# Row products that end quarter by quarter, in a two-block transformer layer on one core

## The reference

```python
# first block
mix = concat([o_a, o_b]) @ w_out
x = x + gate1 * mix
h2 = modulate(rms_norm(x, norm2_gain), shift2, scale2)
y = peer(h2, ...)              # ends in (gates * act) @ expert_up, a sum over 16384 experts
x = x + gate2 * y
# second block
h = rms_norm(x, norm1_gain); proj = h @ w_in; ...
mixed = sigmoid(ga) * (o_hg @ w_hg_out) + sigmoid(gb) * (o_sb @ w_sb_out)
x = x + mixed @ w_o
h2 = rms_norm(x, norm2_gain)
gate, up = split(h2 @ w_ffn_in)
x = x + (silu(gate) * up) @ w_ffn_out
```

## Time and profile before

| | |
|---|---|
| time, median of 3 runs | 1680.39 us (1679.71 to 1683.46) |
| the profiled execution | 1681.05 us, of which its span 1679.3 us |
| PE busy | 1586.3 us, 94% of the span |
| DVE busy | 1226.5 us, 73% |
| ACT busy | 907.7 us, 54% |
| mean granted TensorE clock | 0.979 of full speed |

### The profile page before, as it was taken

How to read it: one execution, slowest core, us unless ns; L and a number is a source line. 1 busy time by engine, 2 the same in 40 slices (tenths; PEclk the granted TensorE clock), 3 DMA queues, 4 the chain that set the end, 5 groups by cost and what they waited for, 6 DMA issues and landing times. The chain is left out here.

```text
span 1679.3 us, 26490 instructions
## 1 busy us (share of the span) xinstructions
PE 1586.3 (94%) x10351; PEld 1426.4 (85%) x10351; DVE 1226.5 (73%) x2476; ACT 907.7 (54%) x1519; POOL 42.7 (3%) x82
## 2 busy tenths in 40 slices
PE   5988889999999999999999999899999899889998
PEld 5976767999999999978888888797888677789997
DVE  5876766889997999957767777657887566654564
ACT  5765455545545555545555555556555756455453
POOL 0022000000000000000000000020000000000000
PEclk9999999999999999999999999999999899999999
DMA  9943354576666454567788777645343223445552
GB/s 322 368 148 115 101 176 132 177 236 231 224 218 206 148 165 149 167 219 241 246 283 289 253 240 239 224 160 167 126 151 126 76 90 111 149 151 178 178 199 101
DMA packets 111664, 313.85 MB, mean 187 GB/s; under 512 B 9440, under 2 KB 10040, under 8 KB 102072
## 3 DMA queue, kind: packets, MB, share of 16 engines
q1 hardware_dynamic: 100008, 276.95, 49.7%
q10 hardware_dynamic: 11040, 33.66, 5.9%
q0 software_dynamic: 496, 1.59, 0.3%
HBM read 293.28 MB, written 18.89 MB: 186 GB/s over the span
## 5 line engine op out<-in xcount | busy, mean ns | idle before, releaser
L300 PE MATMUL ps<-parts,parts 128*128 128x512 f32 (+1 forms) x4992 | 972.7, 357 | 21.1 <-DVE parts L290 15.0
L300 PEld LDWEIGHTS ps<-parts,parts 128*128 128x128 f32 x4992 | 825.7, 192 | 156.1 <-DVE parts L290 15.4
L285 ACT CAST parts<-lead 128x512 fp32r<-128x512 f32 x940 | 579.8, 621 | 618.8 <-PE ps L300 398.5
L290 DVE TENSOR_TENSOR parts<-lead,parts 128x512 fp32r<-128x512 f32 x940 | 641.1, 689 | 330.0 <-ACT parts L285 326.3
L1817 PE MATMUL ps<-parts,parts 128*128 128x256 f32 x3072 | 385.3, 285 | 4.6 <-DVE parts L290 4.6
L1817 PEld LDWEIGHTS ps<-parts,parts 128*128 128x128 f32 x3072 | 372.6, 192 | 5.6 <-DVE parts L290 5.6
L376 PE MATMUL ps<-lead,mem 128*128 128x128 f32 (+2 forms) x292 | 45.5, 319 | 44.9 <-ACT mem L519 23.4
L376 PEld LDWEIGHTS ps<-lead,mem 128*128 128x128 f32 (+2 forms) x292 | 39.8, 159 | 52.6 <-ACT mem L519 24.8
L1994 DVE TENSOR_SCALAR mem<-lead,mem 128x128 f32<-128x128 f32 x256 | 71.0, 340 | 0.0
L1803 PE MATMUL ps<-mem 128*128 128x128 f32 x512 | 67.8, 275 | 0.7 <-DVE mem L1994 0.7
L1803 PEld LDWEIGHTS ps<-mem 128*128 128x128 f32 x512 | 62.8, 192 | 1.1 <-issue 1.1
(11 more groups left out here) (349 smaller groups left out, 999.5 us busy)
## 6 DMA issues: line engine op xcount, KB each, us to landing
lead<-in_peer_expert_down SPq DMA_DIRECT2D x64, 1024.0 KB, 5.5
lead<-in_peer_expert_up SPq DMA_DIRECT2D x64, 1024.0 KB, 6.0
lead<-in_w_in SPq DMA_DIRECT2D x50, 1024.0 KB, 5.1
lead<-in_w_ffn_in SPq DMA_DIRECT2D x22, 1024.0 KB, 5.2
act_spill<-mem ACTq DMA_DIRECT2D x32, 512.0 KB, 5.1
mem<-act_spill ACTq DMA_DIRECT2D x32, 512.0 KB, 3.6
mem<-in_w_ada SPq DMA_DIRECT2D x29, 512.0 KB, 7.5
lead<-in_w_ffn_out SPq DMA_DIRECT2D x11, 1024.0 KB, 4.9
```

The lines of the kernel that those rows point to most:

```text
L285: act.copy(w_hi[g % BUFFERS], st.words(n, u * UNIT, UNIT)).then_inc(hi_ready, 1)
L290: dve.tensor_tensor(w_lo[g % BUFFERS], st.words(n, u * UNIT, UNIT), w_hi[g % BUFFERS].bitcast(F32), ALU.subtract).then_inc(lo_ready, 1)
L300: mm = pe.matmul(o, lhs[a], rhs[b], start=start and i == 0, stop=stop and i == 2, skip_group_check=True, **kw)
```

## The change

A new function `last_units` runs the last 4 units of all five products. It first waits for all four units (`ready`), then does the products in another order: token tile 0, column half 0 (units 0 and 2 of the four); tile 0, half 1 (units 1 and 3); tile 1, half 0; tile 1, half 1. `s_rows` counts the first three quarters, and `unit_used` reaches its last value with the fourth. The second and third of the four buffers are given back together. DVE waits for each quarter and works on 512 columns at a time. `half_roots` replaces `norm_roots` in the three places with a norm: it squares each quarter; the sum of a row's first half, over 1024 and plus the epsilon, becomes the bias of that row tile's root (one small Identity), whose input is the sum of the second half. There is one root for each token tile in place of one for both. ACT waits for its own square and Identity each time. The result is stored in four DMAs of 128 rows x 512 columns in place of two of 128 x 1024.

```diff
+        def half_roots(act, rows, src, s_sq, s_src):
+            steps = 0
+            for tt in range(TT):
+                first, second, base, root = (tiny[:, 8 + 2 * i + tt:9 + 2 * i + tt] for i in range(4))
+                for c, total in enumerate((first, second)):
+                    act.wait_ge(s_src, 2 * tt + c + 1)
+                    act.activation(half_of(rows, tt, c), half_of(src, tt, c), ACT.Square, accum_out=total).then_inc(s_sq, 1)
+                    steps += 1
+                    act.wait_ge(s_sq, steps)
+                    if c == 0:
+                        act.activation(base, first, ACT.Identity, bias=eps, scale=1.0 / D).then_inc(s_sq, 1)
+                        steps += 1
+                one = act.activation(tiny[:, 2 + tt:3 + tt], second, ACT.Sqrt, bias=base, scale=1.0 / D)
+            return one
+
+        def half_of(v, tt, c):
+            return v[:, tt, c * 512:(c + 1) * 512]
+
+        def last_units(pe, ready, half, n, s_rows):
+            order = (0, 2, 1, 3)
+            for i in range(n - 4, n):
+                ready(i)
+            for m, i in enumerate(order):
+                mm = half(n - 4 + i, 0)
+                if m % 2:
+                    mm.then_inc(s_rows, 1)
+            for m, i in enumerate(order):
+                mm = half(n - 4 + i, 1)
+                if m != 1:
+                    mm.then_inc(unit_used, (1, 0, 2, 1)[m])
+                else:
+                    mm.then_inc(s_rows, 1)
...
-                    for i in range(units - 4, units):
+                    def ready(i):
                         if turn and i % 2 == 0:
                             turn.await_k(pe, i // 2)
                         await_unit(pe, g0 + i, 0)
-                        mm = half(i, 0)
-                    mm.then_inc(s_rows, 1)
-                    for i in range(units - 4, units):
-                        half(i, 1).then_inc(unit_used, 1)
+
+                    last_units(pe, ready, half, units, s_rows)
...
                     for tt in range(TT):
-                        if tt == 0:
-                            dve.wait_ge(s_rows, 1)
-                        else:
-                            dve.wait_ge(unit_used, used_value(g0 + units - 1))
-                        dve_part(dve, step, tt)
+                        for c in range(2):
+                            if tt == 0 or c == 0:
+                                dve.wait_ge(s_rows, 2 * tt + c + 1)
+                            else:
+                                dve.wait_ge(unit_used, used_value(g0 + units - 1))
+                            dve_part(dve, step, tt, c)
...
-        def add_mix(dve, step, tt):
-            step(dve.tensor_tensor(at(O_TMP + tt * D, D), product_rows(tt), gate1, ALU.mult))
-            dve.tensor_tensor(x[:, tt, :], x[:, tt, :], at(O_TMP + tt * D, D), ALU.add).then_inc(s_xsum, 1)
+        def add_mix(dve, step, tt, c):
+            gated, o = at(O_TMP + tt * D + c * 512, 512), half_of(x, tt, c)
+            step(dve.tensor_tensor(gated, product_half(tt, c), gate1[:, c * 512:(c + 1) * 512], ALU.mult))
+            dve.tensor_tensor(o, o, gated, ALU.add).then_inc(s_xsum, 1)
...
                 for tt in range(TT):
-                    sp.wait_ge(s_res, tt + 1)
-                    sp.dma_start(out[0, tt * P:(tt + 1) * P, :], x[:, tt, :]).then_inc(s_out, 16)
-                sp.wait_ge(s_out, 16 * TT)
+                    for c in range(2):
+                        sp.wait_ge(s_res, 2 * tt + c + 1)
+                        sp.dma_start(out[0, tt * P:(tt + 1) * P, c * 512:(c + 1) * 512], half_of(x, tt, c)).then_inc(s_out, 16)
+                sp.wait_ge(s_out, 16 * 2 * TT)
```

More of the change, by code:

```diff
@@ L1556, in _, with product_half @@
                     for tt in range(TT):
-                        if tt == 0:
-                            dve.wait_ge(s_rows, 1)
-                        else:
-                            dve.wait_ge(unit_used, used_value(g0 + units - 1))
-                        dve_part(dve, step, tt)
+                        for c in range(2):
[4 more added lines that the diff above has]
+                            dve_part(dve, step, tt, c)
         def product_rows(tt, j=0):
             return psf[:, j * 2048 + tt * D:j * 2048 + (tt + 1) * D]
+        def product_half(tt, c, j=0):
+            return ps[:, 4 * j + 2 * tt + c, :]
         O_TMP = O_C
         s_xsum, s_xsq = sem("x1_rows"), sem("x1_squares")
-        def add_mix(dve, step, tt):
-            step(dve.tensor_tensor(at(O_TMP + tt * D, D), product_rows(tt), gate1, ALU.mult))
-            dve.tensor_tensor(x[:, tt, :], x[:, tt, :], at(O_TMP + tt * D, D), ALU.add).then_inc(s_xsum, 1)
+        def add_mix(dve, step, tt, c):
+            gated, o = at(O_TMP + tt * D + c * 512, 512), half_of(x, tt, c)
+            step(dve.tensor_tensor(gated, product_half(tt, c), gate1[:, c * 512:(c + 1) * 512], ALU.mult))
+            dve.tensor_tensor(o, o, gated, ALU.add).then_inc(s_xsum, 1)
         def sum_roots(act):
             load_roots(act)
-            norm_roots(act, h, x, s_xsq, s_xsum)
+            half_roots(act, h, x, s_xsq, s_xsum)
         s_cols = sem("mods_added")
@@ L1846, in _ @@
                         transposes(pe, [(ps[0:KT, 0, 0:P], mod_cols[:, 5 * KT:6 * KT])]).then_inc(s_gt, 1)
[L1847 to L1852, removed]
+                last_units(pe, lambda i: await_unit(pe, g1 + i, 0), half, 2 * P, s_rows)
             @block.scalar
@@ L2053, in _ @@
                 for tt in range(TT):
[L2054 to L2059, removed]
+                    for c in range(2):
+                        if tt == 0 or c == 0:
+                            dve.wait_ge(s_rows, 2 * tt + c + 1)
+                        else:
+                            dve.wait_ge(unit_used, used_value(g1 + 2 * P - 1))
+                        o = half_of(x, tt, c)
+                        step(dve.tensor_tensor(o, product_half(tt, c, 1), gate2[:, c * 512:(c + 1) * 512], ALU.mult))
+                        dve.tensor_tensor(o, o, half_of(x_back, tt, c), ALU.add).then_inc(s_xsum, 1)
         O_F = O_R + TT * D
@@ L2751, in mix_hg, with add_sb @@
                 step(dve.tensor_tensor(mixed[:, tt, :], product_rows(tt), p2[:, tt, 5 * D:6 * D], ALU.mult))
-        def add_sb(dve, step, tt):
-            step(dve.tensor_tensor(at(O_W + 2048, D), product_rows(tt), p2[:, tt, 6 * D:7 * D], ALU.mult))
-            step(dve.tensor_tensor(mixed[:, tt, :], mixed[:, tt, :], at(O_W + 2048, D), ALU.add))
+        def add_sb(dve, step, tt, c):
+            gated, o = at(O_W + 2048 + c * 512, 512), half_of(mixed, tt, c)
+            step(dve.tensor_tensor(gated, product_half(tt, c), p2[:, tt, 6 * D + c * 512:6 * D + (c + 1) * 512], ALU.mult))
+            step(dve.tensor_tensor(o, o, gated, ALU.add))
         rows_stage("w_sb", n_sbo, 4, n_wo[0] + SLOTS, (x_hi, x_lo), add_sb, Turn("heads", p2[:, :, 2 * D:3 * D]),
@@ L2761, in build, with add_wo @@
         s_xsum, s_xsq = sem("x3_rows"), sem("x3_squares")
-        def add_wo(dve, step, tt):
-            dve.tensor_tensor(x[:, tt, :], x[:, tt, :], product_rows(tt), ALU.add).then_inc(s_xsum, 1)
+        def add_wo(dve, step, tt, c):
+            o = half_of(x, tt, c)
+            dve.tensor_tensor(o, o, product_half(tt, c), ALU.add).then_inc(s_xsum, 1)
         rows_stage("w_o", n_wo, 4, n_ffi[0] + SLOTS, (x_hi, x_lo), add_wo, Turn("mixed_rows", mixed), sum_roots)
@@ L2816, in _ @@
                     half(i, 1).then_inc(unit_used, 1)
[L2817 to L2822, removed]
+                last_units(pe, ready, half, FU, s_rows)
             @block.scalar
@@ L2884, in _ @@
                 for tt in range(TT):
[L2885 to L2889, removed]
+                    for c in range(2):
+                        if tt == 0 or c == 0:
+                            dve.wait_ge(s_rows, 2 * tt + c + 1)
+                        else:
+                            dve.wait_ge(unit_used, used_value(g_o + FU - 1))
+                        o = half_of(x, tt, c)
+                        dve.tensor_tensor(o, o, product_half(tt, c, 1), ALU.add).then_inc(s_res, 1)
 NAMES = ["x", "c", "w_ada", "b_ada", "norm1_gain", "w_in", "attn_q_gain", "attn_k_gain", "attn_rel_bias",
```

## The result

The changed kernel takes 1684.64 us (median of 20 runs, 1683.25 to 1690.12) against 1682.6 us for the kernel before in as many runs (1678.74 to 1685.81). The ratio is **1.0023**, 95% interval 1.0015 to 1.0032: slower, by 3.9 us (2.5 to 5.4). The forecast was +2.8 us and called it no measurable difference. Its edge for that was 0.2%, 3.4 us; the 3.9 lies just beyond it, and the interval takes in both sides. The time of 1684.64 lies in the whole range of the forecast (1679.6 to 1685.2) and 0.1 us outside the forecast's own (to 1684.5). That it lies so near is in part luck: the forecast stands on three runs of the kernel before with a median of 1680.39, and twenty runs have 1682.6.

A forecast was written before the change was run, and what follows sets the result against it. PE, busy 94% of the span, was taken as the bound. Stalls of 8.65 us against 5.33 given back made +3.3, less 0.5 for the clock: 1680.39 + 2.8 = 1683.2 us, own range 1681.0 to 1684.5, whole range 1679.6 to 1685.2.

The forecast's parts named there:

- The stall: At all five product ends, PE waits for the last unit before the last 24 matmuls: 1.73 us each, 8.65 us added.
- the restart: At each product end, PE resuming and the way to the waiting engine take 0.40 us, of which 0.38 was counted.
- The gains: From T to the next stage at five ends, smaller takes, squares, roots and stores give back 5.33 us in all.
- T: The moment at which DVE can take the last rows of a product; forecast to come 1.73 us later.
- The store: End of w_ffn_out: the last store, 256 KB in place of 512 KB, lands 0.5 us sooner, bounds 0 and 1.0.
- The clock: PE's granted clock in the gaps after products: the fall after w_o goes away, so 0.5 us comes back.
- the two long ones: PE's gaps after w_out and expert_up, forecast at 4.8 us each: the clock still falls, costing 1.6 us each.
- the one of 3.8: PE's gap after w_o, forecast to shrink from 4.8 to 3.8 us: the clock rather doesn't fall, 0.5 us back.
- Rival 4: The stall itself lowers the clock in the last 24 matmuls at any one place: up to +5.4 us; chance 0.07.
- Rival 3: At the five product ends the stall costs nothing: 1674.6 us, 0.35% faster; chance 0.06.
- Rival 1: The clock falls at the same three places as before (w_out, expert_up, w_o): 1683.7 us; chance 0.22.
- Rival 2: The clock stays up after w_out or expert_up too: 1681.6 us for one, 1680.0 for both; chance 0.24.

## Why the prediction was nearly right in size and wrong in its verdict

*The stall (forecast 8.65 us for five).* Right in kind and place, a little small. From split to last take it is 7.25 at w_out and 7.36 at w_ffn_out where 7.17 was forecast: four stalls of 1.8 and one of 1.92, 9.1 in all. Each lies above the forecast's upper bound of 1.75. What was mis-sized is the restart, 0.40 at most by the forecast and 0.46 (1.81 less 1.35) here. PE resumes 0.15 us after DVE's low part at w_out and 0.26 at w_ffn_out (1673.63 to 1673.89), where a further wait, for the low parts of the other operand, follows the awaited one; in the earlier trace rows it was 0.05.

*The gains (forecast 5.33).* They were 5.9. The root after w_out ends at T + 2.49 and not T + 2.71, since a following DVE operation starts before its predecessor's recorded end, so that DVE keeps PE's pace; At w_o the root ends at T + 1.77 where T + 1.75 was forecast. The store gave 0.6 for 0.5.

*The sum.* Both errors cancel: +3.3 forecast, +3.24 by the table; that it is so close is luck.

*The clock (forecast: 0.5 us back).* This is the step that failed. "I expect the two long ones to fall still, and the one of 3.8 rather not": the clock fell after w_o as before, and of the 0.5 us only 0.2 came back there (from the first split behind w_o to the last of w_ffn_out 1672.29 - 1485.99 = 186.30 us, before 186.49). And after w_sb, where the forecast had the clock stay up because 2.3 is less than 3.0, and so put nothing into the sum, it fell, for 1.2 us. The forecast judged a gap by its length alone. The runs show that length alone does not decide: 2.25 us behind the early wait brought the clock down in each execution and 2.28 without it in none, and an unchanged gap of 3.1 us did so in seven of twelve. Why the early wait has this effect stays open, as said above. Rival 4 named the stall as a cause of a fall, but looked for it inside the last 24 matmuls; it came one gap later. The Trainium skill (TensorE: Matmul & The Clock Gate, Part 1: The HAM clock gate) ties the clock to how busy PE has been of late and has the moment of a change vary from run to run; the unchanged gap with and without a fall agrees with that.

With the fall the ends come to 3.24 + 1.2 = 4.4 us, inside the measured 2.5 to 5.4. The two spans, 3.5 us apart, can't check this: stretches in which nothing was changed differ by as much. From the first split behind expert_up to the last of w_sb it is 1447.40 - 1088.40 = 359.0 us before and 1447.28 - 1090.67 = 356.6 after, 2.4 less, and the last split of w_out comes at 220.07 for 218.49, 1.6 later.

*The verdict.* The forecast of +2.8 lay 0.6 us under the edge between "the same" and "slower" and gave slower 0.32. With the right clock the terms give 3.3 + 1.2 = +4.5, less the 0.2 of w_o, and the verdict slower. Rival 3 (no stall) fell as a description of this kernel; but a kernel without the stall gained 7.1 us, in the order of what it named. Rival 1 held for its three places and missed the fourth. Rival 2 fell in the profiled executions: the clock stayed up after neither long gap in the changed kernel.

## What to carry to other kernels

When the order of the last tiles is changed, ask of each wait whether it can move as late as its tile is used: here three halves of cover, 2.04 us, were given away five times, and one line's place decided between 0.23% slower and 0.42% faster. A producer that is far from busy can still be late, if a small ring of buffers releases it late. And don't judge an idle gap of TensorE by its length in one trace: the same gap had a fall of the clock in one execution and none in the next, so count the falls over several. Matmuls that nobody reads, put into the gap, are a cheap way to see what the clock costs there.

## What the runs showed of the hardware that was not expected

- A gap of 2.25 us brought the clock down in some executions and one of 3.14 us left it up in another. Where no instruction was changed, a gap of 3.10 to 3.18 us brought it down in seven executions of twelve.
- A fall cost 0.4, 2.4 and 1.2 us behind w_out, expert_up and w_o, and 1.2 to 1.3 behind w_sb.
- The clock also moves where nothing was changed. Early in the program it reads as follows in the profiled execution of before and, below it, of the changed kernel, in the columns of the earlier trace rows:

```profile
21.00:28.00 7.00, 6.25 (x30) 6.28 (x31) 5.74 (x11) 4.25 (x9) 0.00 (x0) 0.51 0.95 353
```

```profile
21.00:28.00 7.00, 5.80 (x33) 5.83 (x34) 6.24 (x12) 4.70 (x10) 0.00 (x0) 1.00 0.92 337
```

  Such falls may be why the twenty runs of either kernel scatter over 7 us; that was not tested. They are why the ends are compared here by distances in the trace.
- Two operations of 512 columns on DVE, one after the other, take 0.66 to 0.73 us from start to start against 1.26 for one of 1024: halving costs 0.1 to 0.2 us a pair.
